# A hybrid recurrent decoder step on one core: who makes the high halves of the input projections' weights, and in what order the down projections start

## What is computed

```python
for l in range(DEPTH):                      # DEPTH = 2
    h = rms_norm(x, norm_mix[l])
    y, s = even_mixer(h, ...) if l % 2 == 0 else odd_mixer(h, ...)
    x = x + y
    h = rms_norm(x, norm_ffn[l])
    y, c = conv_ffn(h, st_conv[l], f_w_up[l], f_conv_w[l], f_conv_b[l], f_w_down[l])
    x = x + y
out = rms_norm(x, norm_final)

# even_mixer:  z = h @ w_in; an mLSTM group and an RWKV-7 group; y = concat(...) @ w_out
# odd_mixer:   z = h @ w_in
#              la = log_sigmoid(a_down @ a_up + a_b) / 16      (decay of the GLA group)
#              a GLA group (q, k, v, la) and an S5 group; y = concat(...) @ w_out
# conv_ffn:    u = h @ w_up; c = causal conv of width 3; y = (val * silu(gate)) @ w_down
```

## Time and profile before

| | before |
|---|---|
| runs: median (lowest to highest of 3) | 1760.52 us (1759.35 to 1769.03) |
| profiled execution: span | 1763.6 us |
| PE busy | 1634.1 us, 93% |
| DVE, POOL, ACT busy | 1053.1, 875.7, 471.8 us |
| mean granted TensorE clock | 0.949 of full speed |
| HBM traffic over the span | 83 GB/s |

### The profile page before, as it was taken

How to read it: one execution, slowest core, us unless ns; L and a number is a source line. 1 busy time by engine, 2 the same in 40 slices (tenths; PEclk the granted TensorE clock), 3 DMA queues, 4 the chain that set the end, 5 groups by cost and what they waited for, 6 DMA issues and landing times. The chain is left out here.

```text
span 1763.6 us, 35383 instructions
## 1 busy us (share of the span) xinstructions
PE 1634.1 (93%) x14910; PEld 1576.0 (89%) x14910; DVE 1053.1 (60%) x1533; ACT 471.8 (27%) x688; POOL 875.7 (50%) x731
## 2 busy tenths in 40 slices
PE   6999996588998999999989998999899999998996
PEld 5999985487987999999989998977799999998996
DVE  4816768747645777776632239676676777765012
ACT  4002123610133343333310031132414333332001
POOL 4666688094013644444376656700374444445763
PEclk8999988688999999999999999998999999999998
DMA  4222111021052222222222222274332222222222
GB/s 176 84 71 83 60 74 54 1 75 56 13 200 69 90 84 83 83 83 83 72 66 88 76 79 60 71 210 139 91 98 77 84 83 83 84 83 61 81 83 88
DMA packets 50679, 149.09 MB, mean 85 GB/s; under 512 B 17552, under 2 KB 19232, under 8 KB 48416
## 3 DMA queue, kind: packets, MB, share of 16 engines
q1 hardware_dynamic: 50592, 147.91, 26.3%
HBM read 127.58 MB, written 19.13 MB: 83 GB/s over the span
## 5 line engine op out<-in xcount | busy, mean ns | idle before, releaser
L280 PE MATMUL PP<-arena_r,dual_r 128*128 128x288 f32 (+1 forms) x6428 | 1116.9, 298 | 39.9 <-POOL dual_r L267 16.2
L280 PEld LDWEIGHTS PP<-arena_r,dual_r 128*128 128x128 f32 (+1 forms) x6428 | 965.3, 190 | 44.3 <-POOL dual_r L267 13.9
L280 PE MATMUL PP<-hT_r,dual_r 128*128 128x288 f32 (+1 forms) x2176 | 647.7, 298 | 0.0
L267 POOL TENSOR_TENSOR dual_r<-w_ring,dual_r 128x1024 fp32r<-128x1024 f32 (+1 forms) x198 | 485.1, 2450 | 17.7 <-ACT dual_r L1962 4.6
L267 POOL TENSOR_TENSOR dual_r<-w_ring,cst 128x1024 fp32r<-128x1024 f32 (+1 forms) x114 | 216.7, 1901 | 408.6 <-PE PP L280 262.2
L280 PEld LDWEIGHTS PP<-hT_r,dual_r 128*128 128x128 f32 (+1 forms) x2176 | 410.5, 189 | 1.3
L270 DVE SCALAR_TENSOR_TENSOR rowbuf<-rowbuf,convp 128x592 f32<-128x592 f32 x176 | 271.3, 1542 | 91.3 <-ACT rowbuf L1985 90.7
L280 PE MATMUL PP<-arena 64*64 64x64 f32 (+6 forms) x3640 | 206.0, 256 | 37.1 <-DVE arena L267 15.3
L280 PEld LDWEIGHTS PP<-arena 64*64 64x64 f32 (+2 forms) x3640 | 182.8, 148 | 57.9 <-issue 32.6
L1962 ACT ACTIVATE dual_r<-w_ring 128x1024 fp32r<-128x1024 f32 x84 | 89.2, 1062 | 332.1 <-PE PP L280 332.1
L267 DVE TENSOR_TENSOR xT<-PP,xT 128x576 f32<-128x576 f32 x32 | 24.2, 758 | 255.5 <-PE PP L280 255.5
(11 more groups left out here) (266 smaller groups left out, 1348.9 us busy)
## 6 DMA issues: line engine op xcount, KB each, us to landing
w_ring<-in_w SPq DMA_DIRECT2D x150, 512.0 KB, 3.5
w_ring<-in_w_down SPq DMA_DIRECT2D x32, 448.0 KB, 3.3
w_ring<-in_w_down SPq DMA_DIRECT2D x16, 512.0 KB, 3.5
xT<-in_x SPq DMA_DIRECT2D x8, 576.0 KB, 7.1
gy_scratch<-dual SPq DMA_DIRECT2D x1, 2304.0 KB, 7.0
dual<-gy_scratch SPq DMA_DIRECT2D x1, 2304.0 KB, 13.7
out_y<-hT SPq DMA_DIRECT2D x4, 576.0 KB
xT<-in_C SPq DMA_DIRECT2D x1, 2064.0 KB, 9.2
```

What stands on the lines that cost most here:

```text
L267: return eng.tensor_tensor(out, a, b, op)
L280: return nc.tensor.matmul(out, lhsT, rhs, start=start, stop=stop)
```

## The change

- In both input projections ScalarE makes the high halves (new helper `high`, a Copy) of all tiles from tile 2 on, and GpSimd only subtracts (`project_low`). Tiles 0 and 1 of each stay with GpSimd. `high` waits for the weights and for the tile before the last. Its calls stand at fixed places between ScalarE's other work.
- `s5_angles` is cut in two parts, behind tile 5 and behind tile 6.
- In the odd layer the evictions of tiles 2 and 3 move into the decay chain, behind the scan of each half; ScalarE does the two Exp in a row, then the two Ln.
- On GpSimd the last `state_out` of the up-projection comes behind slice 0 of down's weights, and the split of the small weights (`wad`) behind slice 1. The first pass of down's loop is written out for that.

The diff, cut to its core:

```diff
             norm(2)
+            high("o_in", "o_hi", 2)
...
             for t in range(2):
-                chain(A(BC[:, t, :], BC[:, t, :], ACT.Exp, scale=-1.0))
+                last = A(BC[:, t, :], BC[:, t, :], ACT.Exp, scale=-1.0)
+            chain(last)
+            for t in range(2):
                 A(BC[:, t, :], BC[:, t, :], ACT.Ln, bias=1.0).then_inc(S("gl_sp"), 1)
+            high("o_in", "o_hi", 3)
             for t in range(2):
+                high("o_in", "o_hi", 4 + t)
                 act.wait_ge(S("gl_kd"), t + 1)
...
-            level_exps(0, 14)
+            for k0, k1, js in ((0, 2, (6,)), (2, 4, (7,)), (4, 6, (8,)), (6, 8, (9,)), (8, 9, (10, 11, 12, 13)),
+                               (9, 11, (14,)), (11, 13, (15,)), (13, 14, ())):
+                level_exps(k0, k1)
+                for j in js:
+                    high("o_in", "o_hi", j)
...
                 chain(V.tensor_tensor_scan(b_, c_("scan128", T), la, 0.0, ALU.mult, ALU.add))
+                evac_z(2 + t)
                 kd = KG[:, t, :]
...
-            evac_z(2)
             diffs(0)
             diffs(1)
-            evac_z(3)
...
+            def project_low(name, sem):
...
+                with pool.Fori(1, RUNS[name][1] // 2) as i:
+                    for s in range(2):
+                        pool.wait_ge(S(sem), 2 * i + (s - 1))
+                        tt(G, w_lo[:, s, :], w_ring[:, s, :], w_hi[:, s, :], ALU.subtract).then_inc(S("w_split"), 1)
...
-                for t in range(2 * FT):
+                for t in range(2 * FT - 1):
                     state_out(t)
...
-            def down(l):
+                return lambda: state_out(2 * FT - 1)
+
+            def down(l, last_state, between=None):
+                c0 = CHUNK0[f"down{l}"]
                 pool.wait_ge(S("proj_done"), USE[f"down{l}"] - 1)
-                pool.wait_ge(S("w_split"), CHUNK0[f"down{l}"])
-                with pool.Fori(0, 4) as i:
-                    chain.loop(i, 6)
+                for e in range(6):
+                    tile, j = e // 3, e % 3
+                    pool.wait_ge(WL[e % 2], 16 * (c0 // 2 + e // 2 + 1))
+                    if e == 2 and between is not None:
+                        between()
+                    if e == 1:
+                        last_state()
+                        pool.wait_ge(S("proj_done"), USE[f"down{l}"])
+                    elif j == 1:
+                        pool.wait_ge(S("proj_done"), USE[f"down{l}"] + tile)
+                    elif e:
+                        pool.wait_ge(S("chunk_used"), 16 * l + 2 * tile + (j == 2) + 1)
+                    chunk(e % 2, DCH[j][1] * P)
...
+            def high(name, sem, j):
+                act.wait_ge(WL[j % 2], 16 * ((CHUNK0[name] + j) // 2 + 1))
+                act.wait_ge(S("proj_done"), USE[name] + j - 1)
+                A(w_hi[:, j % 2, :], w_ring[:, j % 2, :], ACT.Copy).then_inc(S(sem), 1)
...
             A(t_s, l_st, ACT.Exp).then_inc(S("s5_trig"), 1)
+            for j in range(2, 10):
+                high("e_in", "e_hi", j)
             act.wait_ge(S("o_rows"), 1)
...
             A(t_c, t_c, ACT.Sin).then_inc(S("s5_trig"), 1)
+            for j in range(10, 14):
+                high("e_in", "e_hi", j)
             for j in range(12, 16):
+                high("e_in", "e_hi", j + 2)
                 act.wait_ge(FREE[j % 2], j // 2 + 2)
...
             for k in range(14):
                 s = k % 2
+                if k < 12:
+                    high("e_in", "e_hi", 18 + k)
...
-                    if j == 5:
-                        s5_angles()
+                    if j in (5, 6):
+                        s5_angles(j - 5)
```

More of the change, by code:

```diff
@@ L880, in odd_pe, with odd_act @@
             project("o_out", lead=4)
-        def odd_act(act, A, chain, norm, head_norm, split_h):
+        def odd_act(act, A, chain, norm, high, head_norm, split_h):
             norm(2)
+            high("o_in", "o_hi", 2)
             for t in range(2):
@@ L1345, in project @@
                     chain.end_loop(RUNS[name][1] // 2 - first)
+            def project_low(name, sem):
+                first_chunks = 2
+                if name == "o_in":
+                    for s in range(first_chunks):
+                        pool.wait_ge(WL[s], 16 * (CHUNK0[name] // 2 + 1))
+                        pool.wait_ge(S("proj_done"), USE[name] + s - 1)
+                        chunk(s)
+                with pool.Fori(1, RUNS[name][1] // 2) as i:
+                    for s in range(2):
+                        pool.wait_ge(S(sem), 2 * i + (s - 1))
+                        tt(G, w_lo[:, s, :], w_ring[:, s, :], w_hi[:, s, :], ALU.subtract).then_inc(S("w_split"), 1)
             def ffn(l):
@@ L1402, in down @@
                         chunk(e % 2, DCH[j][1] * P)
-                    chain.end_loop(4)
+                    chain.end_loop(3)
             pool.sem_inc(S("chunk_used"), 1)
@@ L1410, in _ @@
                 chunk(s)
-            project("e_in", 1)
+            project_low("e_in", "e_hi")
             s5_turns(pool, chain)
@@ L1420, in _, with small_weights @@
             project("e_out")
[L1421 to L1424, removed]
+            last_state = ffn(0)
+            def small_weights():
+                pool.wait_ge(S("o_small_in"), 32)
+                split(wad, wad_hi, wad_lo, S("small_split"))
+            down(0, last_state, small_weights)
             pool.wait_ge(S("chunk_used"), 17)
-            project("o_in")
+            project_low("o_in", "o_hi")
             pool.wait_ge(S("s5_y"), SP4)
             project("o_out")
-            ffn(1)
-            down(1)
+            down(1, ffn(1))
         @block.tensor
@@ L2210, in _ @@
             split_x(2, "o_in")
-            odd_act(act, A, chain, norm, head_norm, split_h)
+            odd_act(act, A, chain, norm, high, head_norm, split_h)
             split_x(3, "ffn1")
@@ L2367, in row_logs, with s5_angles @@
                 V.tensor_copy(r_mo[:, 1:9], m_s).then_inc(S("ml_rows"), 1)
-            def s5_angles():
-                dve.wait_ge(S("s5_trig"), 1)
-                chain(tt(V, t_a, l_re, t_s, ALU.mult))
-                chain(tt(V, t_b, l_im, t_s, ALU.mult))
-                for out, shift in ((t_s, 0.0), (t_c, np.pi / 2)):
+            def s5_angles(part):
+                if part == 0:
+                    dve.wait_ge(S("s5_trig"), 1)
+                    chain(tt(V, t_a, l_re, t_s, ALU.mult))
+                    chain(tt(V, t_b, l_im, t_s, ALU.mult))
+                for out, shift in (((t_s, 0.0),) if part == 0 else ((t_c, np.pi / 2),)):
                     chain(V.tensor_scalar(t_n, t_b, 1.0 / TWO_PI, shift / TWO_PI, ALU.mult, ALU.add))
```

2 lines of the change are left out of this document (added).

## The result

The changed kernel takes **1751.19 us** (median of 6 runs, 1750.69 to 1753.79). The kernel before, run beside it, took 1766.66 (6 runs, 1759.35 to 1769.03); the ratio is 0.9931, with a 95% interval of [0.9913, 0.995]. In all the comparisons on the chip, this one and four later, the kernel before had medians of 1763.5 to 1766.7 us, so the 1760.52 from which the prediction subtracted came from a low three. Span against span, 1763.6 to 1748.9, the change gives **14.7 us**; forecast were 15.1.

What follows compares the result with a forecast made beforehand. TensorE, busy 93% of the span, was taken as the bound, so only its idle or low-clock time could be won. Terms 3.7 + 8.6 + 2.8 = 15.1 us off 1760.52 gave 1745.4 us; own range 1741 to 1749, wide 1738 to 1752.

Steps and rivals of the forecast that it cites:

- Sum: Whole kernel: savings of 15.1 us, taken off the runs' median of 1760.52, give 1745.4 us.
- for where the median falls: Whole kernel: allowance of 1.5 us in the forecast's own range for the position of the measured median.
- Even input projection: Even input projection: removing its stall and low clock wins 4.5 us, a new stall costs 0.8; net -3.7 us.
- The new stall at tile 2: Even input projection, third tile: ScalarE's later high half makes TensorE wait 0.8 us, bounds 0.3 to 1.5.
- The stall and the dip at 83: Even input projection near 83 us: idle of 2.80 us and 1.7 us lost to lower clock both disappear.
- Odd input projection: Odd input projection: tile 4 starts at 1069.3 instead of 1075.6 at full clock; 6.30 + 2.3 = -8.6 us.
- What could fall late is the weights: Odd input projection: high halves could start late, 0.9 us for tile 7, 0.3 for tile 8; costed at nothing.
- the lockstep rival: Odd input projection: VectorE's 8.7 us per tile delays high halves, six tiles 2.3 us late each; 1769.6 us; chance 0.06.
- The downs: Start of both downs: stalls move behind slice 0, 5.8 and 5.2 us, released by VectorE's low half; -2.8 us together.
- the first rival: Downs: SiLU and products slip in ahead of GpSimd's slice 2, so 17.0 us go; 1731.2 us; chance 0.08.

Runs made afterwards that it cites:

- run 5: Changed kernel with GpSimd's order around both downs, and the small weights' split, as in the kernel before: 1751.35 us.
- run 2: Changed kernel with the angle chain in one piece behind tile 5 again, high halves still on ScalarE: 1749.89 us.
- run 1: Changed kernel with the even input projection's high halves back on GpSimd, angle chain still cut in two: 1758.74 us.
- run 4: Changed kernel with the odd input projection's high halves back on GpSimd, evictions of tiles 2 and 3 still moved: 1753.84 us.
- run 3: Changed kernel with the odd input projection's evictions of tiles 2 and 3 back behind the decay chain: 1751.91 us.
- run 7: Changed kernel, but GpSimd holds each down's slice 2 split back until VectorE has made slice 1's activations ready: 1751.68 us.
- run 6: Changed kernel with only ScalarE's high halves left; angle chain, odd evictions and downs' order as in the kernel before: 1751.77 us.
- run 10: Changed kernel; in downs, slice 1's low half precedes last taps, ScalarE makes slices 1-2 high halves, GpSimd's slice 3 and small-weight splits await all low halves: 1743.18 us.
- run 11: As run 10, with slice 2's copy two places later on ScalarE, angles in one piece, evictions of tiles 2 and 3 behind the decay chain: 1742.76 us.

## Why the prediction was right or wrong

**The time itself** was 5.8 us too low: 1751.19 lies inside the wide range of 1738 to 1752 but outside the forecast's own 1741 to 1749. The step that failed is the one under "Sum": I took the difference off the median of three scattered runs, 1760.52, and allowed 1.5 us "for where the median falls". The runs put that median at 1763.5 to 1766.7, 3 to 6 us higher. Off the profiled execution's own time (span 1763.6, and the changed kernel's runs lie 1.8 us above their profiled span) it would have been 1763.6 + 1.8 - 15.1 = 1750.3, 0.9 us off.

**The sum**, 14.7 against 15.1 us, agrees in part by luck. By stretches of the two timelines the three terms of the forecast give 2.2 + 10.1 + 1.0 = 13.3 us; the other 1.4 came where the code did not change. And each of the three holds a low-clock stretch that comes and goes between kernels whose code there is the same:

```profile
173.70:180.50 6.80, 6.80 (x30) 6.76 (x31) 1.28 (x7) 0.00 (x0) 0.49 (x1) 0.50 0.26 77
```
```profile
174.30:177.60 3.30, 3.30 (x15) 3.27 (x16) 0.57 (x4) 0.00 (x0) 0.00 (x0) 0.50 0.52 159
```

The first row is the changed kernel's, the second that of run 5, which has the same `e_in`; TensorE was busy throughout both.

**Even input projection**, forecast -3.7, is -2.2 at the end of `e_in` (232.22 to 230.05), and -3.9 in run 5 (228.34), so the size was right. The new stall at tile 2 was 0.33 us, inside its bounds, not 0.8. The stall and the dip at 83 went as said. But of the two means that I gave, the cut angle chain did nothing (run 2). And I did not ask what the lighter GpSimd prevents: with both halves on it, the cut alone puts the stall at tile 10 (run 1).

**Odd input projection**, forecast -8.6: from 1038.07 to 1155.09 before, 1035.52 to 1142.46 after, 10.1 us less. Right in the stall (6.30) and its dip (2.3). The rest is chance: the kernel before has a granted 0.52 from 1049.5 to 1053 and the changed one 1.00, but runs 1 and 2, which have the changed kernel's `o_in`, have such a stretch as well and take 108.4 us for it, 8.6 less than before. Here the mechanism failed: I credited the moved evictions. They alone keep a stall of 1.87 us (run 4), and the high halves on ScalarE remove it without them (run 3). "What could fall late is the weights" was rightly costed at nothing: no wait stands between tiles 4 and 15, and the lockstep rival, the one on the slower side, did not occur.

**The downs**, forecast -2.8: -1.0 by the two segments, and -0.4 by the medians of all traces with either order (run 5). The wait was foreseen: the stall moved behind slice 0, VectorE's low half ends it, 6.36 and 5.47 us against forecast 5.8 and 5.2. Slice 1 of down0 starts at 892.25, or 892.25 + 2.54 = 894.8 on the clock of before (604.79 - 602.25 = 2.54), forecast 894.2, and started at 897.4 before. So 2.6 us were gained there, and the lower clock (0.50 from 892.25 to 897.3) took back 2.5, where 1.7 was taken: that is the term of this part that was mis-sized. The near miss of 0.3 us that the first rival needed was one of 0.01 us, but run 7, in which the products run free, shows that a hit would not have paid at down0: there the splits for slice 3 met the low halves, and the segment was 2.4 us longer. At down1 it was 1.5 us shorter, far from what that rival needs for its 17.0 us. That rival should have had next to no chance.

**The rule of the Trainium skill**, *SBUF — State Buffer*, "Who interferes with whom", that the port pair shared by the two engines is locked for a whole instruction of the one that comes first, is what the runs show for VectorE: a 0.24 us operation took 2.26 and ended 0.03 us behind the split it met. For GpSimd I read the rows too mildly. Its split of 1.90 us took 2.42, 0.52 more, beside a tap of 0.84; but the tap had started 0.17 us earlier (883.90 against 884.07), so only 0.67 us of it was left to wait for, and the row is near the Trainium skill's rule.

**Not settled:** how much, if anything, the moved orders add to ScalarE's high halves. Changed kernel and run 6 are 0.6 us apart, less than the runs can tell.

## What to carry to other kernels

Where VectorE and GpSimd share a stretch, count the long GpSimd instructions between the start and the end of VectorE's critical chain, before asking which of its instructions they hit: here each cost the chain 0.9 to 1.8 us, and reordering them moved the stall. Handing them to ScalarE, or holding them back until the whole chain is over, is what shortened it. When a consumer's start is brought forward, look at what its freed buffer lets start, and in whose way that falls. Subtract a forecast difference from the profiled run's own time, not from the median of a few runs that scatter by more than the difference.

## What was unexpected of the hardware

A shorter stall is not followed by less time at the lower clock in proportion, and the same stall not always by the same time. Before, 7.36 us of idle ahead of down0 left some 3 us of it behind TensorE's restart (1.5 us lost, by the prediction's count). After, 6.36 us of idle left 5.05 (892.25 to 897.3, 2.5 lost), and in run 10 2.69 us of idle still left 3 (893.74 to 896.7, 1.5 lost). In run 11, 2.65 us of idle ahead of the same slice left 6.2 (892.82 to 899.0, 3.1 lost). At down1, 5.47 us of idle left 3.3 us in the changed kernel and 5.5 in run 2 (1598.37 to 1603.9), whose code there is the same. Run 11, then run 2:

```profile
892.20:899.00 6.80, 6.18 (x26) 6.21 (x27) 0.47 (x1) 0.00 (x0) 5.08 (x4) 0.50 0.31 81
```
```profile
1597.10:1603.90 6.80, 5.53 (x23) 5.57 (x24) 5.80 (x9) 1.66 (x3) 0.37 (x1) 0.50 0.25 70
```

So at down0 cutting the idle from 7.36 to 2.69 us gave back none of that second price, and one trace does not tell what a stall costs to better than 1.1 to 1.6 us.

The granted clock in the recurrences also differs between kernels whose code there is the same (0.80 and 0.91 from 345 to 420 us, run 5), and the runs of one kernel scatter by 2 to 17 us. The gains of the downs are therefore read from segments as well as from medians.
